# Second gated product at the fifth tap, index half waiting bank by bank, packed weight units and vectors

## The reference

```python
h = rms_norm(x, g_mix[l])
proj = h @ w_in[l]
aq, ak, av, iq, ik, iw, glu_in, cc_in, sb_in, gate_in = jnp.split(proj, offs, axis=-1)
y_a = dsa_attention(qa, ka, va, qi, ki, iw) @ w_oa[l]      # ki from ik, rms_norm with g_kidx
glu_a, glu_b = jnp.split(glu_in, 2, axis=-1)
u = causal_dwconv(glu_a * jax.nn.sigmoid(glu_b), cb_conv_w[l], cb_conv_b[l])   # 31 taps, 512 channels
y_b = jax.nn.silu(layer_norm(u, cb_ln_g[l], cb_ln_b[l])) @ w_ob[l]
merged = gates[0] * y_a + gates[1] * y_b + gates[2] * y_c + gates[3] * y_d
x = x + merged @ w_merge[l]
x = x + (jax.nn.silu(causal_dwconv(h2 @ w_ffn_gate[l], ffn_conv_w[l])) * (h2 @ w_ffn_up[l])) @ w_ffn_down[l]
```

## Time and profile before

| What | Value |
|---|---|
| median of 3 runs | 1773.88 us (1772.96 to 1774.28) |
| the profiled execution's own time | 1773.61 us |
| its span | 1771.8 us |
| PE busy | 1708.9 us, 96% |
| PEld, DVE, ACT, POOL busy | 1612.6, 1220.0, 931.7, 123.9 us |
| chain that ended last | PE 80%, DVE 13%, ACT 3%, DMA 2%, issue 1% |
| DMA | 305.73 MB in 246587 packets, mean 173 GB/s |

### The profile page before, as it was taken

The page is one execution under the profiler, slowest core; times in us unless marked ns, Lnnn a source line. Parts: engine busy times, 40 slices in busy tenths (PEclk is TensorE's granted clock), DMA queues, the critical chain, the costliest instruction groups (busy, mean ns, idle before and its releaser), DMA issues.

```text
span 1771.8 us, 31540 instructions
## 1 busy us (share of the span) xinstructions
PE 1708.9 (96%) x13320; PEld 1612.6 (91%) x13320; DVE 1220.0 (69%) x1928; ACT 931.7 (53%) x1291; POOL 123.9 (7%) x34
## 2 busy tenths in 40 slices
PE   6999999999998999999999999889999999999998
PEld 6999999899888999999999898669998998889986
DVE  7987756797659859467987376968554656666553
ACT  6556564543445556654544366646443655655432
POOL 2702000000005403000000000000000000000000
PEclk9999999999999999999999999999999999999999
DMA  7565445468755655455465554425555575436551
GB/s 246 167 190 166 144 150 207 153 205 222 234 158 163 196 156 165 145 196 194 151 220 192 180 159 123 142 65 170 195 191 192 185 195 153 132 119 213 192 202 71
DMA packets 246587, 305.73 MB, mean 173 GB/s; under 512 B 7218, under 2 KB 221582, under 8 KB 246447
## 3 DMA queue, kind: packets, MB, share of 16 engines
q1 hardware_dynamic: 233911, 289.66, 50.7%
q10 hardware_dynamic: 12536, 14.06, 3.9%
HBM read 299.51 MB, written 4.19 MB: 171 GB/s over the span
## 4 chain that ended last, share of the span: by engine, by line
PE 80%; DVE 13%; ACT 3%; DMA 2%; issue 1%; DVEq 0%; ACTq 0%; SPq 0%
PE psum L481 25%; PE psum L482 24%; PE psum L483 24%; DVE wlo L457 3%; DVE work L1666 1%; DMA raw<-in_b_w_q 1%; DMA raw<-in_a_w_in 1%; DVE psum L1536 1%; ACT work L2620 1%; DVE work L2349 1%; PE psum L2534 1%; DVE work L2333 1%; DVE work L1680 1%; DVE stat L1676 1%; DVE work L1664 1%
## 5 line engine op out<-in xcount | busy, mean ns | idle before, releaser
L449 ACT ACTIVATE whi<-raw 128x2048 fp32r<-128x2048 f32 (+2 forms) x277 | 524.9, 1902 | 376.6 <-PE psum L483 270.3
L457 DVE TENSOR_TENSOR wlo<-raw,whi 128x2048 fp32r<-128x2048 f32 x249 | 566.7, 2281 | 191.1 <-PE psum L483 161.4
L481 PE MATMUL psum<-hT,whi 128*128 128x256 f32 x1890 | 524.8, 278 | 0.0
L482 PE MATMUL psum<-hT,whi 128*128 128x256 f32 x1890 | 524.0, 277 | 0.0
L483 PE MATMUL psum<-hT,wlo 128*128 128x256 f32 x1890 | 523.4, 277 | 0.0
L483 PEld LDWEIGHTS psum<-hT,wlo 128*128 128x128 f32 x1890 | 355.7, 188 | 0.0
L481 PEld LDWEIGHTS psum<-hT,whi 128*128 128x128 f32 x1890 | 355.7, 188 | 0.0
L482 PEld LDWEIGHTS psum<-hT,whi 128*128 128x128 f32 x1890 | 355.3, 188 | 0.0
L457 POOL TENSOR_TENSOR wlo<-raw,whi 128x2048 fp32r<-128x2048 f32 (+1 forms) x28 | 122.7, 4395 | 561.3 <-ACT whi L449 392.9
L481 PE MATMUL psum<-whi,hidden 128*128 128x512 f32 x352 | 137.3, 390 | 1.0 <-issue 1.0
L483 PE MATMUL psum<-whi,hidden 128*128 128x512 f32 x352 | 137.0, 389 | 0.0
(11 more groups left out here) (384 smaller groups left out, 3328.9 us busy)
## 6 DMA issues: line engine op xcount, KB each, us to landing
raw<-in_w_in SPq DMA_DIRECT2D x76, 1024.0 KB, 5.4
raw<-in_ffn_w_up SPq DMA_DIRECT2D x44, 1024.0 KB, 5.1
raw<-in_w_ffn_gate SPq DMA_DIRECT2D x22, 1024.0 KB, 5.4
raw<-in_w_ffn_up SPq DMA_DIRECT2D x22, 1024.0 KB, 5.6
raw<-in_w_ffn_down SPq DMA_DIRECT2D x22, 1024.0 KB, 4.8
raw<-in_ffn_w_down SPq DMA_DIRECT2D x22, 1024.0 KB, 4.9
raw<-in_b_w_q SPq DMA_DIRECT2D x12, 1024.0 KB, 6.4
raw<-in_a_w_in SPq DMA_DIRECT2D x10, 1024.0 KB, 5.3
```

What stands on the lines that cost most here:

```text
L449: act.activation(part(whi, n, HIGH_SLOTS), part(raw, n, RAW_SLOTS), ACT.Copy).then_inc(high_made, 1)
L457: eng.tensor_tensor(part(wlo, n, LOW_SLOTS), part(raw, n, RAW_SLOTS), part(whi, n, HIGH_SLOTS).bitcast(F32), ALU.subtract).then_inc(stream ...
L481: nc.tensor.matmul(dst, left[0], right[0], start=first, stop=False)
L482: nc.tensor.matmul(dst, left[0], right[1], start=False, stop=False)
```

## The change

Four things change.

1. In both layers of the first block, the second gated product stands behind tap 3 of the first convolution and ahead of the fifth tap; before it stood behind ten taps.
2. PE's unit 4 waits for bank 0 before j = 0 and for bank 1 only before j = 1.
3. The weights arrive from the host as an array `weights` of 274 x 128 x 2048, in which a unit's partition is one contiguous run (8 KB for a full unit), where before a partition took eight runs of 1 KB, four of 2 KB or two of 4 KB. The bytes that are read stay the same.
4. The small vectors arrive as an array `parameters` of 128 x 1584 (811 KB), already turned and spread. One DMA on ACT's queue loads it into `par`, and one of 128 x 8 loads the first gain. The rows in `praw`, POOL's clearing, PE's eight transposes, DVE's three copies and 17 of SP's 19 small transfers go. DVE waits for the load (`side_load`) where `copy_parameters` stood. The new function `packed_parameters` fills the array on the host, with the same columns in `par` as before and the gains and the bias behind them.

```diff
+def packed_weights(units):
...
+    out = np.zeros((len(units), P, UNIT), np.float32)
+    for n, (w, _) in enumerate(units):
+        kt, cols = w.shape[0] // P, w.shape[1]
+        out[n, :, 0:kt * cols] = w.reshape(kt, P, cols).transpose(1, 0, 2).reshape(P, kt * cols)
...
-            soon = [(cst[:, 2 * P:], consts[:, 2 * P:]),
-                    layer_rows(0, 0, a["cb_conv_w"].rearrange("l k (t p) -> (k t) l p", p=P))]
+            soon = [(cst[:, 2 * P:], consts[:, 2 * P:]), (par[:, :], params)]
             later = []
...
                 act.dma_start(cst[:, 0:2 * P], consts[:, 0:2 * P]).then_inc(ident_load.sem, 16)
-                act.wait_ge(operand_ready.sem, operand_ready.at(1))
-                act.dma_start(early[0:KT, :], a["g_mix"][0].rearrange("(t p) -> t p", p=P)).then_inc(gain_load.sem, 16)
-                act.wait_ge(operand_ready.sem, operand_ready.at(2))
+                act.dma_start(first_gain[:, :], params[:, R_MISC(0) + M_MIX:R_MISC(0) + M_MIX + KT]) \
+                   .then_inc(gain_load.sem, 16)
...
                         if half == 0:
                             whole_turned(pe)
-                            own_bank(p)
-                            own_bank(p + 1)
                         for j in range(TT):
+                            if half == 0:
+                                own_bank(p + j)
...
                 for n in range(count):
                     dense(n)
-                    if l == 0 and n == 1:
-                        turn_parameters(pe)
...
                 if l == 0:
-                    copy_parameters(dve)
+                    dve.wait_ge(side_load.sem, side_load.at(side_loads[0]))
                 for b in range(4):
                     whole_low(dve, hT, turned, norm_gain, b)
                 glu_gate(1)
-                long_conv(0, 0, 10)
+                long_conv(0, 0, 4)
                 glu_product(1)
-                long_conv(0, 10, 18)
-                long_conv(0, 18, LONG)
+                long_conv(0, 4, LONG)
...
-                    sp.dma_start(part(raw, n, RAW_SLOTS).rearrange("p (k c) -> p k c", k=kt),
-                                 src.rearrange("(k p) c -> p k c", p=P)).then_inc(raw_landed[n % RAW_SLOTS], 16)
+                    sp.dma_start(part(raw, n, RAW_SLOTS), weights[n, :, 0:kt * cols]) \
+                      .then_inc(raw_landed[n % RAW_SLOTS], 16)
...
-                        sp.wait_ge(operand_ready.sem, 2)
```

More of the change, by code:

```diff
@@ L142, in spread, with packed_parameters, put @@
     return bass.AP(ap.tensor, ap.offset, dims[:dim] + [[0, n]] + dims[dim:])
+PAR, HEAD_GAIN, IDX_GAIN, GATE_BIAS = (n * P for n in (0, PARAM_TILES, PARAM_TILES + 2 * DEPTH, PARAM_TILES + 2 * DEPTH + 1))
+PARAM_COLS = GATE_BIAS + 3 * QH
+def packed_parameters(a):
+    rows = np.zeros((PARAM_TILES * P, P), np.float32)
+    def put(at, values):
+        v = values.reshape(-1, P)
+        rows[at:at + v.shape[0]] = v
+    for l in range(DEPTH):
+        put(R_LONG(l), a["cb_conv_w"][l])
+        for at, name in ((M_GATE, "b_gate"), (M_MIX, "g_mix"), (M_FFN, "g_ffn"), (M_CB, "cb_conv_b"),
+                         (M_LNG, "cb_ln_g"), (M_LNB, "cb_ln_b"), (M_CC, "cc_conv_w")):
+            put(R_MISC(l) + at, a[name][l])
+        put(R_FFC(l), a["ffn_conv_w"][l])
+    for at, name in ((M2_MIX, "norm_mix_2"), (M2_FFN, "norm_ffn_2"), (M2_KV, "kv_norm_2"), (M2_PEK, "a_pe_k_2"),
+                     (M2_PEV, "a_pe_v_2")):
+        put(R_PART2 + at, a[name])
+    out = np.zeros((P, PARAM_COLS), np.float32)
+    out[:, PAR:HEAD_GAIN] = rows.T
+    out[:, HEAD_GAIN:IDX_GAIN] = np.stack([a["g_qa"], a["g_ka"]], 1).reshape(1, -1)
+    out[:, IDX_GAIN:IDX_GAIN + DEPTH * IDX_DIM] = a["g_kidx"].reshape(1, -1)
+    out[:, GATE_BIAS:PARAM_COLS] = a["a_b_gate_2"].reshape(1, -1)
+    return out
+def packed_weights(units):
[3 more added lines that the diff above has]
+        out[n, :, 0:kt * cols] = w.reshape(kt, P, cols).transpose(1, 0, 2).reshape(P, kt * cols)
+    return out
 class Signal:
@@ L231, in weight_units, with two_part_transformer @@
     return u
-def two_part_transformer(nc, a, consts, onehots, out):
+def two_part_transformer(nc, a, unit_shapes, weights, params, consts, onehots, out):
     ctx = ExitStack()
@@ L397, in two_part_transformer @@
         stream = Stream()
-        stream.units = [(src, src.shape[0] // P, src.shape[1], e) for src, e in weight_units(a)]
+        stream.units = [(n, kt, cols, e) for n, (kt, cols, e) in enumerate(unit_shapes)]
         for _, _, _, e in stream.units:
@@ L772, in setup_stage @@
             return base
-        def turn_parameters(pe):
-            pe.wait_ge(side_load.sem, side_load.at(side_loads[0]))
-            pe.wait_ge(root_spread.sem, root_spread.at(1))
-            for n in range(PARAM_TILES):
-                mm = nc.tensor.transpose(bank(2 + n // 4)[:, (n % 4) * P:(n % 4 + 1) * P], praw[:, n, :], ident)
-            mm.then_inc(side_full.sem, 1)
         def load_distances(act):
@@ L794, in distance_row @@
               .then_inc(distance_full.sem, 1)
-        def copy_parameters(dve):
-            dve.wait_ge(side_full.sem, side_full.at(1))
-            dve.tensor_copy(par[:, 0:4 * P], bank(2))
-            v_link(dve.tensor_copy(par[:, 4 * P:PARAM_TILES * P], bank(3)[:, 0:(PARAM_TILES - 4) * P]))
         def copy_distance(dve, base, n):
@@ L2850 @@
     nc = _bacc.Bacc("TRN2", target_bir_lowering=False, num_devices=1, dynamic_dma_scratch_size=2048)
+    inputs = {name: _np.asarray(v) for name, v in inputs.items()}
+    units = weight_units(inputs)
     arrays, aps = {}, {}
@@ L2856 @@
     extra = []
-    for name, v in (("shape_constants", shape_constants()), ("distance_tables", distance_tables())):
+    for name, v in (("weights", packed_weights(units)), ("parameters", packed_parameters(inputs)),
+                    ("shape_constants", shape_constants()), ("distance_tables", distance_tables())):
         arrays[f"in_{name}"] = v
@@ L2860 @@
     out = nc.dram_tensor("out_dram", [1, S, D], F32, kind="ExternalOutput").ap()
-    two_part_transformer(nc, aps, extra[0], extra[1], out)
+    shapes = [(w.shape[0] // P, w.shape[1], engine) for w, engine in units]
+    two_part_transformer(nc, aps, shapes, *extra, out)
     r = _run(nc, [arrays], core_ids=[0])
```

56 lines of the change are left out of this document (8 added, 48 removed).

## The result

| | before | after |
|---|---|---|
| median | 1773.42 us (1772.42 to 1774.28, 4 runs) | 1762.04 us (1761.30 to 1763.07, 4 runs) |
| span of the profiled execution | 1771.8 us | 1759.5 us |

The changed kernel takes 0.9936 of the time (95% interval 0.9925 to 0.9948), 11.4 us less. 1761.2 us was forecast. One figure of the text ahead has to be mended: there are 277 weight units, not 274, as the 272, 4 and 1 issues of the profile add up to; no term used it.

What follows compares the result with a forecast made beforehand. PE, busy 96% of the span, was taken as the bound. Minus 6.7 (layer 0), 7.0 (layer 1) and 0.7 (packed rows), plus 1.7 (start), make minus 12.7: from 1773.9 to 1761.2 us, range 1757.0 to 1768.5.

Steps and rivals of the forecast that it cites:

- The holes: Before unit 4: PE's idle times of 6.73 and 4.94 us go; unit 5 ends 8.6 and 7.0 us earlier.
- The new limit in layer 0: Before unit 14: PE stands 1.9 us for ACT behind DVE, so layer 0 keeps 6.7 us.
- The cast: DVE's cast of positions, layer 0: due at 62.1 us, waits for POOL only to 62.5; room 1.2 us.
- the rival: "The cast meets POOL": layer 0's cast waits for unit 11's `wlo`, to 67.9 us; total 1768.1 us; chance 0.17.
- The start: Loading `par` beside x delays PE's first work: plus 1.7 us, between 2.2 in full and 0 or a 0.3 gain.
- the minus 0.2 of the rival: At the start: `par` runs behind x, so plus 1.7 becomes minus 0.2 us; total 1759.3 us; chance 0.15.
- Packed rows: 8 KB weight rows: minus 0.7 us in dilated attention (0 to minus 1.1), 0 in compressed attention.
- The table's term: Bias table in compressed attention beside long weight rows: taken as 0, between minus 0.8 and plus 1.0 us.
- the table later than DVE needs it: Compressed attention: a sign of being wrong, the bias table that DVE adds coming too late; no size given.
- The gain comes back: DVE's selection of keys does not move with PE, both layers' 13.7 us return; total 1774.9 us; chance 0.07.
- packed rows move badly: Weight loads with 8 KB rows fall below 191 GB/s; at half of 346, about 1880 us; chance 0.06.
- x is not delayed: At the start: `par` starts late enough to run behind x; total 1759.3 us; chance 0.15.

Runs made afterwards that it cites:

- e4: The changed kernel with unit 4 waiting for both banks up front again; 1765.03 us, ratio 0.9955.
- e6: The changed kernel with ACT's copy of the second convolution and the square root behind the eviction of unit 12; 1762.21 us, ratio 0.9936.
- e8: The changed kernel with ACT's copy and square root behind unit 12's eviction, and its squares ahead of the `whi` copy that waits for weights; 1761.38 us, ratio 0.9930.
- e13: The changed kernel measured once more, without edits; 1760.21 us, ratio 0.9926.
- e7: The changed kernel with two extra DVE copies of 512 columns (1.4 us) ahead of layer 0's cast of the positions; 1768.93 us, ratio 0.9966.
- e5: The changed kernel with `par` loaded by SP behind the third weight unit instead of by ACT at the start; 1761.22 us, ratio 0.9930.
- e10: The changed kernel with the compressed-attention bias table issued in two halves, behind units 1 and 2, and the two small weights behind unit 3; 1758.53 us, ratio 0.9914.
- e14: The changed kernel, meant to read compressed attention's full weight units in 1 KB rows, but only units 171 to 177 were shortened; 1762.15 us, ratio 0.9936.
- e2: The kernel before with only the weights packed into long rows; 1772.72 us, ratio 0.9996.
- e1: The kernel before with only the second gated product moved ahead of the fifth tap and unit 4 waiting bank by bank; 1761.86 us, ratio 0.9933.
- e3: The kernel before with only the small vectors in one transfer at the start; 1775.06 us, ratio 1.0014.
- e12: The changed kernel with the edits of e8, e5 and e10 together, and the two small weights issued ahead of the table; 1756.74 us, ratio 0.9902.

## Why the prediction was right

- **The holes.** Right. Unit 6 started 7.15 us earlier after a start 1.23 us later, so 8.4 us against 8.6. Layer 1 gave 7.1 and 7.2 us against 7.0. Unit 4 started without an idle time, the clock window is at 1.00, and e4 shows the bank-by-bank wait to be worth the 1.6 us that was worked out for each layer.
- **The new limit in layer 0.** Right in mechanism and size: DVE's end, ACT behind it, and 2.13 us of idle time before unit 14, 1.9 forecast. Not seen was that a second limit lies right behind it, the squares (e6, e8): the chain named was not the only one. The 2.13 us hold at PE's faster pace (2.15 in e13); at the slower one the wait is 0.95 to 0.98, and the layer takes the same time, 152.8 to 152.9 us from unit 6 to its end.
- **The cast.** Forecast (with the start's 1.7 us added) for 63.8 us, waiting to 64.2 for POOL, next `wlo` at 65.0. Measured: 63.89, 64.18, 64.73. The 1.2 us of room were 0.84. e7 put the rival into effect and it cost 6.9 us by the medians, the number of the text. That it is the very number is in part luck: the trace has 6.4 us in layer 0, and the second median of the changed kernel would make it 8.7.
- **The start.** `par` beside x cost 1.23 us, less than 1.7, and more than the minus 0.2 of the rival; e5 took it away again. Over all profiles, the nine kernels that load `par` beside x started unit 1 at 22.90 to 23.52 us and the five that don't at 21.42 to 22.17, 1.45 us between the averages. The bound of 2.2 us was too high by its own rows: `par`'s 0.81 MB less the taps' 0.13 are 0.68 MB, not 0.77, and 2.0 us at 346 GB/s. The 0.4 us of the transposes came as forecast at unit 2, which started 0.81 us later where unit 1 had started 1.23 later; at the end of unit 3 PE was 1.09 us later (40.83 against 39.74), so 0.1 was left.
- **Sum of start and layer 0**: plus 1.7 less 6.7 is minus 5.0; measured minus 4.8. Both terms were 0.5 to 0.6 us too large in size, and the errors cancel, which is luck. In the three other profiles with the same start and the same layer 0 the sum is near: minus 4.9 (e13), 5.5 (e10) and 5.6 (e14).
- **Packed rows.** The terms were minus 0.7 (dilated attention) and 0 (the table). Measured in the changed kernel: 1.2 us lost from 773 to 1214 us and 1.7 won up to 1540, minus 0.4 in all. The table's term was mis-sized: beside long rows it is later, 1.8 us more at the sums where 1.0 was the bound. The 1.2 us are not its measure, since 1.5 of them are the longer stretch of low clock ahead of it. In dilated attention the size was right and the place was wrong. The wait that the prediction named, before 1471.20, does not go with the rows: it is 0.66 us in e2 and 0.72 in e13, with long rows, and 0.63 in e1 with short ones. What long rows removed is a wait of 0.75 us one step earlier, for ACT behind a weight unit, in the kernel before:

```profile
1436.17 1.92 ACT L449 ACTIVATE whi<-raw 128x2048 fp32r<-128x2048 f32 x1 [7.86 <-DMA raw<-in_b_w_q]
```

```profile
1438.71 0.36 PE L481 MATMUL psum<-query_rows,whi 128*128 128x256 f32 x1 [0.75 <-ACT work L2605]
```

  It is 0.41 and 0.21 us in the two others with short rows (e1, e3) and in none of the eleven kernels with long rows. e2 won 1.0 us at this place and the changed kernel 0.9. Part of the 1.7 us is the kernels' spread: from 1214 to 1540 us the two others with short rows show 0.8 and 1.0, the eleven with long rows 1.4 to 2.1. e2 says that table and bands together are nothing that can be measured.
- **The signs.** One of the signs of being wrong did show, "the table later than DVE needs it": DVE waited 8.94 us where it had waited 7.18, and PE 4.05 where it had 2.29. In the second profile of the changed kernel (e13) PE did not wait at the sums.
- **The rivals.** "The gain comes back" and "packed rows move badly" did not show. "x is not delayed" fell with 12.41 in the timeline.

## What to carry to other kernels

Moving an order by a few instructions, with one wait split in two, was worth 11.7 us, and the two data layouts beside it nothing or a loss; run such parts alone before crediting them. Work out for each gain which wait stands next on the same chain, and expect a further one behind that: e6 removed one wait and got nothing, e8 removed two and got 2.6 us in its layer, of which the time of the whole program showed nothing. A long DMA issued by an engine that also evicts can hold that engine for 9 to 14 us; issue it in pieces, between evictions, and early.

## What the runs showed of the hardware

**A tiny cast on DVE ends when POOL's tensor_tensor ends.** In all fourteen kernels profiled (before, after and twelve more) the cast of 2 columns ended 0.02 to 0.03 us after a `wlo` on POOL, and took 0.29 to 4.24 us by how long that one still had to run. DVE's tap instructions ran beside POOL undisturbed (54 in 21.25 us, 0.39 us each, while POOL's run of five went on). The Trainium skill (SBUF — State Buffer, section SBUF: two separate sides) describes an exclusive lock on a port pair that DVE and POOL share; the rows agree for the cast, and the taps show that not every DVE instruction has to wait.

**ACT's DMA issue can take far longer behind others.** The first issues of the table took 0.31 and 0.51 us; the small weights behind it, 64 KB each, took up to 8.7 us (e6). Issued ahead of the table they took 0.41 and 0.49 (e12). That the queue was full when an issue took long fits this, and is not shown.

**PE's pace at full granted clock had two values.** From one matmul to the 24th behind it in units 6 to 13, PE took 2.74 us in the changed kernel and 2.84 in e10, with the clock at 1.00 and no idle time in both (second fence):

```profile
58.94 0.28 PE L517 MATMUL psum<-whi,hT_first 128*128 128x256 f32 x1
61.67 0.28 PE L517 MATMUL psum<-whi,hT_first 128*128 128x256 f32 x1
```

```profile
58.48 0.28 PE L517 MATMUL psum<-whi,hT_first 128*128 128x256 f32 x1
61.32 0.28 PE L517 MATMUL psum<-whi,hT_first 128*128 128x256 f32 x1
```

Of the fourteen profiles eight show the first pace there and six the second (e1, e5, e6, e10, e12, e14). In layer 0 the slower pace cost nothing, since DVE set the end: the wait before unit 14 was 0.98 us instead of 2.13. Its cause is open.
